# Moving a sliding-window attention between the weight chunks of the product that feeds it, in a two-block layer on one Trainium2 core

## The reference, cut to what matters

```
h   = rmsnorm(x, mix_pre_gain)
q,k,v,rq,rf,ri,rg = split(h @ w_in)                  # 2048 -> 1024+128+128+4*1024
A   = sliding_window_attention(q, k, v, sinks)       # 16 heads of 64, 2 kv heads, window 128, ALiBi
Rn  = hgrn2_chunkwise(rq, rf, ri, rg, ...)           # 8 heads of 128, gated linear recurrence
x  += rmsnorm(concat(rmsnorm(A)*gain, Rn) @ w_out)   # A is normed over its 1024 channels
x  += rmsnorm(relu(rmsnorm(x) @ w_up)^2 @ w_down)
```

## Time and profile before

| what | value |
|---|---|
| three runs | 3166.66 us median, 3163.67 to 3179.24 |
| profiled execution, its own time | 3179.61 us |
| its span (first to last instruction) | 3177.8 us, 1.8 us of its time lie outside |
| busy in the span | PE 88%, DVE 61%, ACT 40%, POOL 4% |
| input product of block 2 (`g_p`) | 1871.6 to 2118.5 us of the span |
| mixing stage after it, barrier to barrier | 2120.1 to 2303.8 us |
| output product `g_o2` starts on PE | 2313.7 us |

### The profile page before, as it was taken

How to read it: one execution, slowest core, us unless ns; L and a number is a source line. 1 busy time by engine, 2 the same in 40 slices (tenths; PEclk the granted TensorE clock), 3 DMA queues, 4 the chain that set the end, 5 groups by cost and what they waited for, 6 DMA issues and landing times.

```text
span 3177.8 us, 46110 instructions
## 1 busy us (share of the span) xinstructions
PE 2795.9 (88%) x19726; PEld 2432.7 (77%) x19726; DVE 1950.2 (61%) x2537; ACT 1285.5 (40%) x1740; POOL 113.0 (4%) x145
## 2 busy tenths in 40 slices
PE   2378996998988899999999999976589999999998
PEld 2367785877877888888888888865478888888887
DVE  5877663766654577667666655547655646556564
ACT  1143343323214555445445454446255444343343
POOL 0111101111000000000000000000000000000000
PEclk9989996888888899999999999988799999999998
DMA  8645661322215266767566535520063555555552
GB/s 326 234 168 203 212 212 53 100 87 93 84 64 198 94 208 190 238 199 238 198 199 191 178 129 192 186 90 1 0 225 120 199 185 186 185 186 186 186 185 92
DMA packets 278892, 516.57 MB, mean 163 GB/s; under 512 B 9792, under 2 KB 101952, under 8 KB 278432
## 3 DMA queue, kind: packets, MB, share of 16 engines
q1 hardware_dynamic: 275456, 500.21, 47.1%
q0 software_dynamic: 2800, 10.36, 0.9%
q10 hardware_dynamic: 432, 3.06, 0.2%
HBM read 511.36 MB, written 2.10 MB: 162 GB/s over the span
## 4 chain that ended last, share of the span: by engine, by line
PE 77%; DVE 10%; ACT 6%; issue 5%; DMA 1%; DVEq 0%; POOL 0%; ACTq 0%; POOLq 0%
PE ps L649 42%; PE ps L651 21%; DVE ACCa L1451 3%; PE ps L601 2%; PE ps L786 1%; PE ps L781 1%; PE ps L771 1%; PE ps L968 1%; DVE WLb L1468 1%; PE ps L674 1%; PE ps L930 1%; ACT WHb L1032 1%; PE ps L587 1%; DVE MX L1526 1%; PE ps L738 1%
## 5 line engine op out<-in xcount | busy, mean ns | idle before, releaser
L649 PE MATMUL ps<-XB,WHb 128*128 128x512 f32 x2304 | 821.8, 401 | 23.7 <-DVE WLb L1468 19.7
L1468 DVE TENSOR_TENSOR WLb<-RAWb,WHb 128x2048 fp32r<-128x2048 f32 (+1 forms) x196 | 427.2, 2192 | 366.7 <-ACT WHb L1032 366.4
L651 PE MATMUL ps<-XB,WLb 128*128 128x256 f32 x2304 | 648.6, 282 | 0.0
L649 PEld LDWEIGHTS ps<-XB,WHb 128*128 128x128 f32 x2304 | 438.2, 190 | 129.2 <-issue 13.8
L1032 ACT ACTIVATE WHb<-RAWb 128x2048 fp32r<-128x2048 f32 (+1 forms) x196 | 356.7, 1833 | 416.6 <-PE ps L651 414.8
L1468 DVE TENSOR_TENSOR WLd<-RAWd,WHd 128x2048 fp32r<-128x2048 f32 x144 | 328.4, 2291 | 320.4 <-ACT WHd L1032 320.4
L649 PE MATMUL ps<-XD,WHd 128*128 128x512 f32 x1280 | 457.5, 401 | 16.3 <-DVE WLd L1468 16.3
L651 PEld LDWEIGHTS ps<-XB,WLb 128*128 128x128 f32 x2304 | 440.1, 191 | 0.0
L1032 ACT ACTIVATE WHd<-RAWd 128x2048 fp32r<-128x2048 f32 x144 | 274.4, 1914 | 357.8 <-PE ps L651 355.8
L649 PE MATMUL ps<-FB,WHd 128*128 128x512 f32 x1024 | 362.3, 399 | 0.0
L651 PE MATMUL ps<-XD,WLd 128*128 128x256 f32 x1280 | 359.9, 281 | 0.0
(11 more groups left out here) (310 smaller groups left out, 3664.4 us busy)
## 6 DMA issues: line engine op xcount, KB each, us to landing
RAWb<-in_ffn_w_in SPq DMA_DIRECT2D x168, 512.0 KB, 5.0
RAWd<-in_w_up SPq DMA_DIRECT2D x64, 1024.0 KB, 5.2
RAWd<-in_w_down SPq DMA_DIRECT2D x64, 1024.0 KB, 5.1
RAWa<-in_ada_w SPq DMA_DIRECT2D x48, 1024.0 KB, 5.1
RAWa<-in_rwkv_w_rkv SPq DMA_DIRECT2D x48, 1024.0 KB, 5.2
RAWb<-in_w_in SPq DMA_DIRECT2D x40, 1024.0 KB, 5.0
RAWb<-in_ffn_w_out SPq DMA_DIRECT2D x36, 1024.0 KB, 5.2
RAWs<-in_ada_w SPq DMA_DIRECT2D x32, 1024.0 KB, 5.0
```

Of the source, the lines that this page charges most:

```text
L649: pe.matmul(bank[:, :], WH[tag][:, w, o:o + P], acts(k), start=(k == 0), stop=False)
L651: mm = pe.matmul(bank[:, 0:T], WL[tag][:, w, o:o + P], acts(k)[:, 0:T], start=False, stop=last)
L1468: dve.tensor_tensor(WL[tag][:, n % WN, 0:size], RAW[tag][:, slot, 0:size], WH[tag][:, n % WN, 0:size].bitcast(F32), ALU.subtract).then_inc ...
```

## The change

It reorders the tiles of `g_p`, lets it use six banks instead of seven, and calls hooks: PE has one in the middle and one at the end of every chunk, ACT and DVE one per chunk that takes two steps. From group 2 on, one single stream of `heads()` advances by one step per hook (four steps to a head, 66 steps for 16 heads; there are 72 hooks). The attention uses banks 6 and 7. Its bias is made on DVE from one distance tile of 128 KB (`DIST`) and a slope per head; the factor 0.125 goes into the norm of k. Its buffers lie in `R`, which is free then; the result goes back into the q tiles of `PJ`.

After the barrier `hgrn()` runs alone, with banks 0 to 5 for its products. Within a level the order on DVE becomes decay, masks of the level before, weighting. The sigmoid and one silu are done in g_p's last group. The attention's norm goes between the first levels. The output norm is made for tokens on the partitions: 16 matmuls of one column, one 128 by 16 reciprocal, 16 broadcasts of it, four multiplications. SP loads w_out's first chunks after barrier 4 instead of 5; `RAWd` is laid behind `WHd` and `WLd`, so that it does not overlap the stage's buffers.

```diff
-        segs = [[(i, min(4, NP_ - i))] for i in range(0, NP_, 4)]
+        p_tiles = [8, 9] + list(range(8)) + list(range(18, 26)) + list(range(10, 18)) + list(range(26, NP_))
+        p_groups = [p_tiles[i:i + 4] for i in range(0, NP_, 4)]
...
+                b = (i - gm.tile0) % 6 if gm is g_p else i % 7
...
-            return banks[6 + G_USES.index(name) % 2]
+            return banks[G_USES.index(name) % 6]
...
-                   ("d", end_p, end_m, 5)]
+                   ("d", end_p, end_m, 4)]
...
-                                if k == 0 and i >= 7:
-                                    pe.wait_ge(s_ev, i - 6)
+                                if k == 0 and tile_before[i] is not None:
+                                    pe.wait_ge(s_ev, tile_before[i] + 1)
...
+                            if hook and kk_ == 1 and len(ch["ks"]) == 4:
+                                hook(g, ci, 0)
...
+            def heads():
+                for n in range(66):
+                    h = n // 4
+                    tile, hp, g, sl = h // 2, h % 2, h // 8, h % 2
+                    if n % 4 == 0 and h < 16:
...
+                            pe.wait_ge(*hA(h - 1, "pt"))
+                        pe.wait_ge(s_ps, p_place[tile] + 1)
+                        pe.matmul(banks[6][:, 0:128], PJ[:, tile, 0:P], KD[:, g, hp, 0:P], start=True, stop=True)
+                        pe.matmul(banks[6][:, 128:384], PJ[:, tile, P:2 * P], KD[:, g, hp, :], start=True,
+                                  stop=True).then_inc(hP.sem, 1)
+                    if n % 4 == 3:
+                        pe.wait_ge(*hA(h, "pr"))
...
+                            mm = pe.transpose(banks[6][:, m * P:(m + 1) * P], SS[:, sl, m * P:(m + 1) * P], ident)
...
+                    if n % 4 == 1 and h:
...
+                        pe.wait_ge(*hA(p, "pt"))
...
+                for li in range(2, 8):
+                    decay(li)
+                    for g4 in range(4):
+                        masked(f"L{li - 1}_{g4}", g4, li - 2, f"L{li - 2}_{g4}" if li > 2 else f"d{g4}")
+                    weighted(li)
...
+                dve.wait_ge(*gP(0, "n3"))
+                dve.tensor_scalar(HN[:, :], banks[7][:, 0:16], 1.0 / 128, 1e-6, ALU.mult, ALU.add).then_inc(gV.sem, 1)
+                dve.wait_ge(*gA(0, "rt"))
+                dve.reciprocal(HN[:, :], HN[:, :]).then_inc(gV.sem, 1)
+                for step in range(4):
...
+                    dve.tensor_tensor(o, o, b2(banks[step]), ALU.mult)
...
-            pool.dma_start(BI[:, :, :], A["alibi"]).then_inc(s_bi, 16)
+            pool.dma_start(DIST, A["dist"]).then_inc(s_di, 16)
...
+            pool.wait_ge(s_ps, 1)
             pool.dma_start(KD[64:128, 0, 1, :], PJ[0:64, 8, :]).then_inc(s_kd, 16)
```

More of the change, by code:

```diff
@@ L151, in two_blocks @@
             g_f.append((f1, plan_gemm(A["ffn_w_out"][0], quads, list(range(a, b)))))
-        segs = [[(i, min(4, NP_ - i))] for i in range(0, NP_, 4)]
+        p_tiles = [8, 9] + list(range(8)) + list(range(18, 26)) + list(range(10, 18)) + list(range(26, NP_))
+        p_groups = [p_tiles[i:i + 4] for i in range(0, NP_, 4)]
+        p_place = {tile: i for i, tile in enumerate(p_tiles)}
+        segs = []
+        for tiles in p_groups:
+            runs = []
+            for tile in tiles:
+                if runs and tile == sum(runs[-1]):
+                    runs[-1] = (runs[-1][0], runs[-1][1] + 1)
+                else:
+                    runs.append((tile, 1))
+            segs.append(runs)
         g_p = plan_gemm(A["w_in_2"][0], segs, list(range(ND)))
@@ new lines, in beside_p, with hook @@
+            def beside_p():
+                slots = heads()
+                def hook(g, ci, half):
+                    if g == 1 and ci == 0 and half:
+                        over_rows("p")
+                    if g == 1 and ci == 3 and half:
+                        take7()
+                        pe.wait_ge(s_ps, 2)
+                        for n in range(2):
+                            mm = pe.transpose(banks[7][:, n * P:(n + 1) * P], PJ[:, 9, n * P:(n + 1) * P], ident)
+                        mm.then_inc(s_vtp, 1)
+                    if g > 1:
+                        next(slots, None)
+                return hook
@@ L1209, in stage_s, with heads @@
                 yield
-            def heads(k):
-                tiles, base = head_streams[k]
-                for n, tile in enumerate(tiles):
-                    for hp in range(2):
-                        hq, s = 2 * tile + hp, base + hp
-                        sm, sink = SM[:, hq, :], vec("attn_sinks_2", hq, 1)
-                        yield
-                        yield
-                        act.wait_ge(*hV[k](n, f"nm{hp}"))
-                        act.activation(SS[:, s, 0:128], SS[:, s, 0:128], ACT.Exp, bias=sm[:, 0:1],
+            def heads():
+                for n in range(66):
+                    h = n // 4
+                    sl = h % 2
+                    if n % 4 == 0 and h < 16:
+                        sm = SM[:, h, :]
+                        act.wait_ge(*hV(h, "nm"))
+                        act.activation(SS[:, sl, 0:128], SS[:, sl, 0:128], ACT.Exp, bias=sm[:, 0:1],
@@ new lines, in hgrn @@
+                for li, h in levels[2:]:
+                    exps(li, h)
+                for step in range(4):
+                    o = R[:, 8 + 2 * step:10 + 2 * step, :]
+                    act.wait_ge(*gP(0, f"o{step}"))
+                    act.activation(o, b2(banks[6]), ACT.Copy)
+                    act.activation(DE[:, 0, 512 * step:512 * step + 512], banks[6][:, :],
+                                   ACT.Square).then_inc(gA.sem, 1)
+                act.wait_ge(*gV(0, "rs"))
+                act.activation(HN[:, :], HN[:, :], ACT.Sqrt).then_inc(gA.sem, 1)
```

533 lines of the change are left out of this document (257 added, 276 removed).

## The result

The changed kernel takes 3143.3 us in the median of five runs (3138.8 to 3150.1), the kernel before, in the runs made beside it, 3177.6. The ratio is 0.9905, with a 95% interval of 0.9876 to 0.9934: faster by some 30 to 34 us. I had forecast 3123.5 and a gain of 43. The profiled execution took 3138.86 us and its span is 3137.1, against 3177.8 before.

The account below looks back on a forecast made before the run. PE alone bounds g_p; the stage after it is a chain of waits. g_p grows 39.1 us, the stage falls from 183.7 to 102, g_o2 starts 0.5 earlier: -43 from 3166.7 gives 3123.5 us, range 3105 to 3146.

Parts of the forecast that it names:

- the boundary of groups: At g_p's group ends: PE stalls 0.65 us for its bank at nine boundaries, +5.9 us, bounds 0 and 12.
- The sum paragraph: Whole kernel: 39.1 + 102 - 183.7 - 0.5 = -43 us, taken from the median 3166.7, giving 3123.5 us.
- my own timetable: A head's chain in g_p: ACT 2.4 us late for its next weight copy, whose weights are wanted over 11 us later.
- a sign of being wrong: In g_p: the forecast would be wrong if a group takes over 30 us.
- The visits on PE: In g_p: attention's scores, transposes and products with v add 32.8 us of PE time, and 0.4 for v's transposes.
- The stage alone: Barrier to barrier after g_p: 102 us instead of 183.7, of which 6 for the clock; ends 96 and 118.
- The start of g_o2: After the stage: w_out's chunks are there earlier, so PE starts the second output product 0.5 us earlier.
- Clock stays up: Stage alone: pauses of 3 us are harmless, stage 96 us, kernel 3117.5 us; chance 0.15.
- Clock falls in every pause: Stage alone: half clock after every pause and to the end, stage 118 us, kernel 3139.5 us; chance 0.12.
- PE waits at its visits: In g_p: each of 48 attention visits finds its semaphore 0.5 us late, +24 us, kernel 3147.5 us; chance 0.09.
- The attention holds back the weights: In g_p: a waiting head delays weight copies and PE starves; 64 us more, kernel 3187 us; chance 0.05.
- Masks late: Stage's start: SP's 4 MB load delays the masks, sums start at 14 instead of 8, kernel 3127 us; chance 0.04.

Follow-up runs that it names:

- e12: The changed kernel once more, with no edit: 3136.6 us in the median of six runs.
- e1: Changed kernel, but DVE does a group's adds and norms before the weights' subtraction at the last chunk of a g_p group: 3131.1 us.
- e3: Changed kernel with both orders at g_p's group ends: ACT evacuates before copying the probabilities, DVE adds before the subtraction: 3124.4 us.
- e4: Changed kernel with the attention left out altogether on PE, ACT and DVE; output not the reference's: 3085.5 us in one run.
- e9: Changed kernel plus unread identity products on PE: 20 after the barrier, 11 ahead of each level, 3 ahead of the broadcasts: 3138.6 us in one run.
- e7: Changed kernel with the output norm as before the change, all-ones product and four reciprocals of 3.34 us: 3158.1 us in one run.
- e6: Changed kernel, but from the third level on DVE takes the masks of the level before ahead of the decay: 3169.1 us in one run.
- e11: Changed kernel with the diffs of e3 and e10 together: 3114.5 us in the median of six runs.
- e10: On top of e9, the scan's mask is loaded early, beside the input product: 3129.7 us in one run.

## Why the prediction was off

The sign was right and 3143.3 lies inside the range (3105 to 3146), but near its end, which I had set there for a slow clock and late visits and not for what happened: that part is luck. The point was 19.8 us too low: 10.9 from the base, 8.9 from a gain of 34.3 in the medians in place of 43. In the profiles the gain missed by 13.3, and nearly all of it is one step, the boundary of groups.

**The base.** The sum paragraph says that the profiled execution of before was 13 us above the median shown, and takes the gain from the median, 3166.7. In the three later sets, 19 runs of before, its medians were 3175.5 to 3176.5. The three runs shown held two of the shorter ones, and the profiled one was the ordinary case. From 3179.6 my own sum would have given 3136.5. This is 10.9 us of the miss.

**The boundary of groups**, the step that failed: 5.9 us in the sum, bounds 0 and 12. It measured 18.5 (15.6 against e12), seven stalls of 1.77 us and the clock after some of them. The step reads "DVE adds (0.42): free at 1.95 us": it took DVE as free, from the earlier trace rows, where DVE had waited 0.72 for ACT. But my own timetable, one paragraph above, said that ACT is late for its next weight copy, and I costed that at nothing since PE wants these weights 11 us later. PE does; DVE does not wait so long. Its subtraction stands ahead of the additions, it now starts when the late copy ends, and so it runs across the group's end. With the subtraction out of the way (e1) the stall is 0.61 us, the 0.65 that I had worked out for ACT's side, and a group takes the 27.3 us of my forecast; in the changed kernel it takes 28.4 to 28.6, and 30.1 in the three with the slow clock, past the 30 that I had named as a sign of being wrong. The late copy was found and its first victim was not: the step asked when the data are wanted, not what is queued behind the instruction that waits for them. The second term that was missing is the clock, some 6 us, which fell after three of these stalls in a stage that I had priced at 1.00 throughout.

**The visits on PE**, 32.8 + 0.4, measured 32.6 (e3 less e4). The parts differ and cancel, which is luck: from starts to starts in e3's timeline, with what the next pair is longer by, three transposes cost 0.33 (0.25 of it from 1982.14 to 1982.39), not 0.55; scores 0.65 for 0.75; the product with v 0.99 for 0.75. The 0.55 of the earlier trace rows is a busy time, and most of it lies under the products that follow: the record at 1967.08 above says 0.49, and the next product starts 0.24 us after it.

**The stage alone**, 102, measured 103.6. By the same milestones, from the barrier: decay of level 2 at 31.8 (I had 32); end of the last weighting 76.8 (74); last mask 83.0 (79); output steps 94.3 (90); end 103.6 (96, before the clock). Of the 7.6 us above 96 the clock has some 7: two slow levels (8.53 and 8.41 for 7.0) cost 2.9, the last burst 1.4, the broadcasts 2.7. I had given the clock 6. e9 shows the stage with most of it taken out. The start of g_o2 measured 0.6 earlier for 0.5.

**The rivals.** *Clock stays up*: not by itself, since four of seven bursts were slow; with e9's extra products it does for the levels, and its 96 is about right. *Clock falls in every pause*: not either. After pauses of some 3.1 us between one (e4, e7) and five (e1) of the seven bursts were slow; after 7.4 us all were (e6). The output steps, which my 118 had at half clock, kept their 2.78 us. The Trainium skill's page "TensorE: Matmul & The Clock Gate", section "HAM oscillation", has every burst begin slow in a kernel whose waits are longer than its bursts. That is so here only in e6, and there the trace agrees. *PE waits at its visits*: no wait of PE in g_p has the attention as its releaser; 0.5 us at each was out by all of it. *The attention holds back the weights*: the lateness is real, ACT's 111.7 us behind the maxima and DVE's 54.2 behind the copies show it, but a head stayed inside its two chunks and PE never waited for WLb. It showed at the group's end, in DVE's order. *Masks late*: DVE waited 8.0 us for the mask of the sums, and e11 shows that this costs nothing.

## What to carry to other kernels

When a copy or a conversion ahead of time becomes late on an in-order engine, don't ask when its result is wanted but what stands behind it in that engine's program: here an urgent addition of 0.4 us stood behind an unhurried subtraction of 2.3, and the two in the other order were worth 9 to 12 us, with the other engine's order 16 to 18.5, by which profile of the changed kernel they are held against. Two engines in line must be put right together: the one that isn't last gives nothing alone. And where two profiles or three runs of a kernel differ by more than the effect sought, take the sum from the profiled execution and compare stretch by stretch.

## What was not expected of the hardware

In stretches in which PE never idles and the granted clock is 1.00 in both, the same code ran at one of two rates. The groups of instructions on PE from 2620 to 3020 us, in the changed kernel's profile and then in e12's, which is the same kernel:

```profile
L668 PE MATMUL ps<-FB,WHd 128*128 128x512 f32 x512 | 181.0, 399 | 0.0
```
```profile
L668 PE MATMUL ps<-FB,WHd 128*128 128x512 f32 x512 | 177.6, 391 | 0.0
```

A pair takes 0.353 us in the one and 0.346 in the other (400 us over 1133 and 1155 pairs), 2% apart. Of the 14 profiles six, those of before and of the changed kernel among them, had the longer pitch there and eight the shorter, nothing between; and from g_o2's start to the end they took 863 to 867 us or 853 to 855. The rate belongs to a stretch and not to a run: from 1720 to 1760 us, in the first block, before and the changed kernel had 0.347 and e12 had 0.353, the other way round than later. Gaps of some 12 us between runs of one kernel (e12's at 3134 to 3137 and at 3147 and 3150) would fit this, but only one run of each kernel has a trace, so that is not shown. What sets the rate no run here shows; it is not the chip, since four profiles from one chip had both (e9 and e10 to e12).

The second is that a pause does not decide the clock by its length: seven pauses of 3.05 to 3.16 us were followed by four slow bursts in the changed kernel's profile and by one in e7's. With 2.6 us of unread products in the pause none of seven was slow (e9), in e10 and e11 one.
